# Expert weights in 16 KB pieces: neighbouring rows to one partition, and one DMA for each 2 MB slot

## What is computed

```python
def expert_choice_ffn(h, w_router, w1, w3, w2):        # h (1, 256, 1024)
    cap = EC_CAPACITY_FACTOR * N // N_EXPERTS           # 32 tokens for each of 16 experts
    aff = softmax(h @ w_router)
    gate, idx = top_k(swapaxes(aff, 1, 2), cap)
    xg = h[bidx, idx]                                   # (16, 32, 1024)
    a = einsum('becd,edf->becf', xg, w1)                # w1, w3: (16, 1024, 2048)
    b = einsum('becd,edf->becf', xg, w3)
    ye = einsum('becf,efd->becd', silu(a) * b, w2) * gate   # w2: (16, 2048, 1024)
    return zeros_like(h).at[bidx, idx].add(ye)
```

## Time and profile before

| what | value |
|---|---|
| median of 3 runs | 2690.86 us |
| lowest and highest | 2688.85 and 2696.54 us |
| the profiled execution | 2689.66 us, of which the span of the trace is 2687.9 us |
| TensorE busy | 2231.6 us (83% of the span) |
| TensorE weight loads | 1647.2 us (61%) |
| VectorE, ScalarE, GpSimd busy | 633.4, 588.1, 860.6 us |
| DMA | 680.04 MB, mean 253 GB/s |
| issue to landing of a 1 MB expert load, median | 23.1 us (to the ring), 20.7 us (to the arena) |

### The profile page before, as it was taken

The page is one execution under the profiler, slowest core; times in us unless marked ns, Lnnn a source line. Parts: engine busy times, 40 slices in busy tenths (PEclk is TensorE's granted clock), DMA queues, the critical chain, the costliest instruction groups (busy, mean ns, idle before and its releaser), DMA issues.

```text
span 2687.9 us, 34816 instructions
## 1 busy us (share of the span) xinstructions
PE 2231.6 (83%) x15124; PEld 1647.2 (61%) x15124; DVE 633.4 (24%) x1233; ACT 588.1 (22%) x656; POOL 860.6 (32%) x211
## 2 busy tenths in 40 slices
PE   6799899766665666766665999998998999998998
PEld 2568666422222222222222998997997998997996
DVE  4213332311111111111113033433112032433111
ACT  1111210000000000000001443533333443443332
POOL 1000000000000000000002765676786766576785
PEclk9889799777778778877786999999999999999999
DMA  9634123699999999999997744465554744455553
GB/s 331 191 135 165 62 77 125 265 418 418 418 418 418 419 416 417 417 419 418 418 418 267 266 147 141 130 177 172 188 182 163 240 148 150 126 169 185 174 187 125
DMA packets 284793, 680.04 MB, mean 253 GB/s; under 512 B 11788, under 2 KB 164374, under 8 KB 251217
## 3 DMA queue, kind: packets, MB, share of 16 engines
q1 hardware_dynamic: 282001, 671.55, 67.3%
q0 software_dynamic: 2400, 6.41, 1.0%
q10 hardware_dynamic: 288, 0.53, 0.1%
HBM read 673.85 MB, written 4.59 MB: 252 GB/s over the span
## 4 chain that ended last, share of the span: by engine, by line
PE 63%; DMA 20%; SPq 10%; DVE 4%; issue 1%; ACT 1%; DVEq 0%; ACTq 0%
PE bank L1607 62%; DMA ring_sb<-w_exp 17%; SPq L571 10%; DMA arena_sb<-w_exp 2%; PE bank L1610 2%; DVE x_sb L951 1%; DVE arena_sb L951 1%; DVE arena_sb L954 1%; DVE x_sb L954 1%; DMA ring_sb<-w_in 1%; DMA arena_sb<-hy_skip 0%; DVE x_sb L1450 0%; DMA ring_sb<-w_ada 0%; DVE sm_sb L1438 0%; ACT arena_sb L789 0%
## 5 line engine op out<-in xcount | busy, mean ns | idle before, releaser
L658 POOL TENSOR_TENSOR ring_parts<-ring_sb,ring_parts 128x2048 fp32r<-128x2048 f32 x186 | 849.5, 4576 | 1463.1 <-ACT ring_parts L844 1462.6
L1607 PE MATMUL bank<-hT_parts,ring_parts 128*128 128x256 f32 x3520 | 648.0, 286 | 5.9 <-DVE arena_parts L951 5.9
L1607 PE MATMUL bank<-arena_parts,ring_parts 128*128 128x256 f32 x2672 | 611.2, 284 | 0.0
L1607 PE MATMUL bank<-ring_sb,arena_sb 128*32 128x512 f32 (+2 forms) x2848 | 410.6, 682 | 203.2 <-DMA ring_sb<-w_exp 188.8
L1607 PE MATMUL bank<-arena_sb 128*32 128x256 f32 (+10 forms) x3038 | 434.7, 478 | 161.2 <-DMA arena_sb<-w_exp 121.6
L1607 PEld LDWEIGHTS bank<-hT_parts,ring_parts 128*128 128x128 f32 x3520 | 556.8, 194 | 9.0 <-DVE arena_parts L951 7.5
L1607 PEld LDWEIGHTS bank<-arena_sb 128*128 128x128 f32 (+4 forms) x3038 | 256.4, 172 | 325.6 <-DMA arena_sb<-w_exp 165.0
L1607 PEld LDWEIGHTS bank<-arena_parts,ring_parts 128*128 128x128 f32 x2672 | 450.9, 193 | 0.5 <-issue 0.5
L844 ACT CAST ring_parts<-ring_sb 128x2048 fp32r<-128x2048 f32 x186 | 350.3, 1887 | 270.6 <-DMA ring_sb<-w_ffn_down 66.9
L1607 PEld LDWEIGHTS bank<-ring_sb,arena_sb 128*32 128x32 f32 (+1 forms) x2848 | 112.6, 136 | 478.9 <-DMA ring_sb<-w_exp 293.6
L951 DVE TENSOR_TENSOR arena_sb<-bank,arena_sb 128x512 f32<-128x512 f32 (+5 forms) x205 | 127.2, 643 | 939.8 <-PE bank L1607 875.5
(11 more groups left out here) (208 smaller groups left out, 1022.9 us busy)
## 6 DMA issues: line engine op xcount, KB each, us to landing
ring_sb<-w_exp SPq DMA_DIRECT2D x256, 1024.0 KB, 23.1
arena_sb<-w_exp SPq DMA_DIRECT2D x128, 1024.0 KB, 20.7
ring_sb<-w_in SPq DMA_DIRECT2D x112, 1024.0 KB, 5.3
ring_sb<-w_ada SPq DMA_DIRECT2D x24, 1024.0 KB, 14.1
ring_sb<-w_ffn_gate SPq DMA_DIRECT2D x22, 1024.0 KB, 5.3
ring_sb<-w_ffn_up SPq DMA_DIRECT2D x22, 1024.0 KB, 5.3
ring_sb<-w_ffn_down SPq DMA_DIRECT2D x22, 1024.0 KB, 4.8
ring_sb<-w_ret_proj SPq DMA_DIRECT2D x16, 1024.0 KB, 5.9
```

The lines of the kernel that those rows point to most:

```text
L658: g.tensor_tensor(low, half(n)[0], high.bitcast(F32), ALU.subtract).then_inc(s["lo_ready"], 1)
L1607: return M.matmul(o, l, r, start=first, stop=last)
```

## The change

All three expert tensors go to the partitions in another order. Of w1 and w3, rows 8p to 8p + 7 go to partition p, so that a slot holds two neighbouring rows, 16 KB in one piece; the next partition's piece lies 64 KB further in memory. Of w2, slot r holds rows 512r + 4p to 512r + 4p + 3 in partition p, 16 KB in one piece, and the slot as a whole is 2 MB of memory without a gap. Each slot is one DMA, and the semaphore's counts are halved.

The sums over features stay the same only if the other operand comes in the same order. So the reads on TensorE take a stride: `gather` and `h2T` read `xn2` at every eighth feature, the transposes of `hact` at every fourth, and the halves of `ada_turn` that feed this layer at every eighth. The router's weights are loaded in the same order (one 512-byte piece to a partition), and two rows of constants are put in that order ahead of the launch.

```diff
-        E1 = a["w_exp1"][0].rearrange("e (k p) f -> e p k f", p=P)
-        E3 = a["w_exp3"][0].rearrange("e (k p) f -> e p k f", p=P)
-        E2 = a["w_exp2"][0].rearrange("e (k p) f -> e p k f", p=P)
+        E1 = a["w_exp1"][0].rearrange("e (p k) f -> e p k f", p=P)
+        E3 = a["w_exp3"][0].rearrange("e (p k) f -> e p k f", p=P)
+        E2 = a["w_exp2"][0].rearrange("e (r p c) f -> e r p c f", p=P, c=4)
...
-                w, r = ((E1, c), (E3, c - 4), (E2, c - 8))[c // 4]
                 n = 2 if c < 8 else 4
-                src = w[e, :, n * r:n * r + n]
-                m = n // 2
-                for h in range(2):
-                    sp.dma_start(expert_slot(c, n)[:, h * m:(h + 1) * m],
-                                 src[:, h * m:(h + 1) * m]).then_inc(expert_landed[c % XRING], 16)
+                src = E2[e, c - 8] if c >= 8 else (E1, E3)[c // 4][e, :, 2 * (c % 4):2 * (c % 4) + 2]
+                sp.dma_start(expert_slot(c, n), src).then_inc(expert_landed[c % XRING], 16)
...
-                             (w_router, a["w_router"][0].rearrange("(k p) c -> p k c", p=P)),
+                             (w_router, a["w_router"][0].rearrange("(p k) c -> p k c", p=P)),
...
-                    ins = mm(b[:, 2 * c:2 * c + 2], adarow[:, c // 4, (c % 4) * P:(c % 4 + 1) * P], selsum[:])
+                    row = adarow[:, 2 * (c // 8):2 * (c // 8) + 2].rearrange("p a b -> p (a b)")
+                    by_rows = 2 * batch + c // 8 in (3, 4)
+                    ins = mm(b[:, 2 * c:2 * c + 2], row[:, c % 8:D:8] if by_rows else row[:, (c % 8) * P:(c % 8 + 1) * P], selsum[:])
...
-            turn("h2T", xn2)
+            for i in range(4):
+                b = open_unit("h2T", i)
+                for j in range(2):
+                    for t in range(2):
+                        ins = tr(b[:, j * T + t * P:j * T + t * P + P], xn2[:, t, 2 * i + j:D:8])
+                close(ins)
...
-                        ins = mm(bank[1][:, d * CAP:(d + 1) * CAP], xn2[:, t, d * P:(d + 1) * P], sel[:, t], t == 0, t == 1)
+                        ins = mm(bank[1][:, d * CAP:(d + 1) * CAP], xn2[:, t, d:D:8], sel[:, t], t == 0, t == 1)
...
-                    pe.wait_ge(expert_landed[c % XRING], 32 * (c // XRING + 1) + e * (32 * PER_EXPERT // XRING))
+                    pe.wait_ge(expert_landed[c % XRING], 16 * (c // XRING + 1) + e * (16 * PER_EXPERT // XRING))
...
-                    ins = tr(bank[2][:, c * P:(c + 1) * P], hact[:, c * P:(c + 1) * P])
+                    ins = tr(bank[2][:, c * P:(c + 1) * P], hact[:, c:512:4])
```

More of the change, by code:

```diff
@@ L1919, in expert @@
                     m = 8 + r
-                    pe.wait_ge(expert_landed[m % XRING], 32 * (m // XRING + 1) + e * (32 * PER_EXPERT // XRING))
+                    pe.wait_ge(expert_landed[m % XRING], 16 * (m // XRING + 1) + e * (16 * PER_EXPERT // XRING))
                     w = expert_slot(m, 4)
@@ L2194 @@
     b_in, b_in_2 = arrays["b_in"][0], arrays["b_in_2"]
+    by_rows = lambda v: v.reshape(-1, P, KD).transpose(0, 2, 1).reshape(-1, P)
+    b_ada = rows["b_ada"].reshape(6, D)
+    rows["b_ada"] = np.concatenate([b_ada[0:3].reshape(-1, P), by_rows(b_ada[3:5]), b_ada[5:6].reshape(-1, P)])
+    rows["norm_ffn_g"] = by_rows(rows["norm_ffn_g"])
     packs = {
```

## The result

The changed kernel takes 2672.35 us in the median of 6 runs (2667.63 to 2673.97), the kernel before 2691.65 us in the median of 6 (2685.78 to 2703.37). The ratio is 0.9919, with a 95% interval from 0.9899 to 0.9939: 19 us faster, and clear of the 0.3% that a change must pass to be told from none. The forecast was 2670 us, in a range of 2664 to 2685. The profiled execution of the changed kernel took 2673.63 us, with a span of 2671.8 us.

The account below looks back on a forecast made before the run. The expert stage was taken as bound by the 16 DMA engines' pace through bytes and pieces. -23.2 + 3 = -20.2 us from 2689.66 gives 2669.5; with 1.2 us for the median 2670.7, said as 2670 us, range 2664 to 2685.

Parts of the forecast that it names:

- the line: Expert stage: a 2 MB slot takes 4.824 us plus 9.3 ns for each piece an engine moves.
- 16 KB pieces: Expert stage: 4.898 us a slot, saving 9.0 us on w1 and w3 and 14.2 on w2, -23.2 us.
- Rival A: Expert loads: nothing won beyond 8 KB pieces, so -6.5 us in sum, 2684 us; chance 0.13.
- One DMA for a slot: SyncE's issues of expert loads: 192 fewer, but no landing moves, 0 us.
- The strided reads ahead of the stage: TensorE's 80 loads in h2T, gather(0) and one turn's worth of ada_turn: +3 us, between 0 and +13.9.
- paces part of these: gather(0), 0.220 against 0.113 us a product: something besides the load paces part of the 13.9 us, hiding slower loads.
- rival B: Strided stationary blocks on TensorE load at half pace: +13.9 us, -9.3 us in sum, 2682 us; chance 0.13.
- the +3 us: Cost taken for strided reads ahead of the experts, a fifth of the +13.9 us upper bound.
- The gathers in the loop: gather(e + 1) in the expert loop: even 10.3 us instead of 5.14 is covered by queued loads, 0 us.
- Behind the stage: Chain after the last landing: nothing of the change in it, so all the stage saves is handed on.
- C: w1 and w3 pieces 64 KB apart meet in one part of memory: slower, up to +43 us, 2734 us; chance 0.10.
- D: Something behind the expert stage gives the saving back, leaving around 2690 us; chance 0.06.

Follow-up runs that it names:

- the gapless slots: Changed kernel with slot c of w1 and w3 holding rows 256c + 2p and 256c + 2p + 1, TensorE reading at stride two: 2671.31 us, ratio 0.9920.
- the pitch of 1 MB: Changed kernel with w1 and w3 read 1 MB apart from partition to partition instead of 64 KB, for timing alone: 2673.04 us in one run.

## Why the prediction was right, by its own steps

**The bound.** The stage was bound by the DMA engines, and stays so: share 1.02 before the change and 1.01 behind it. Its length, with the 3.9 us taken from the kernel before, followed the line in nine other versions, within 0.7 us, from 914 to 984 us.

**16 KB pieces.** Forecast 4.898 us a slot and -23.2 us; measured 4.895 us in the slots shown and -23.9 us in the stage of two single executions. The line read from 2, 4 and 8 KB held at 16 KB. Rival A (nothing beyond 8 KB) would have left 4.97 us.

**One DMA for a slot.** Forecast 0, measured 0 (0.9991, and the same stage to 0.1 us).

**The strided reads ahead of the stage.** Forecast +3 us between 0 and 13.9. In the rows of the changed kernel, `gather(0)` is 7.82 us instead of 7.03, turning `xn2` 3.33 instead of 3.27, the second batch's turn 7.33 instead of 6.97, and the third's 7.17 instead of 3.63: +4.8 us; in two other versions with the same strides the third took 6.01 and 5.83 us, which makes 3.4 to 3.6 us. So the size was right. But its reason was only half right. A strided block starts every 7.70 / 32 = 0.24 us at both clock levels; a contiguous one every 0.113 us at 2.4 GHz and every 0.22 us at 1.2 GHz, which was the granted clock (0.50) in `gather(0)` both before and after. TensorE's windows show it, with the number of products in parentheses and the granted clock behind it. The first row is `gather(0)` of the changed kernel, the second lies in its gather(1):

```profile
504.00:512.00 8.00, 7.77 (x32) 0.50 0.01 2
533.00:535.00 2.00, 2.00 (x10) 1.00 1.04 442
```

The same in the kernel before, `gather(0)` and gather(1):

```profile
497.00:503.00 6.00, 6.00 (x30) 0.50 0.01 3
524.00:526.00 2.00, 2.00 (x20) 1.00 1.03 410
```

In 2 us at 2.4 GHz stand 10 strided products against 20 contiguous ones. What "paces part of these" was the clock, and rival B's doubling is true at the high clock and nearly nothing at the low one. So the +3 us, taken as a fifth of the bound without a row for it, came right in part by luck: it rests on `gather(0)` running at 1.2 GHz. At 2.4 GHz its 32 blocks alone would have cost 32 x (0.24 - 0.113) = 4 us, by estimate from these rows, instead of 0.8. The rule on lines in the Trainium skill ("SBUF — State Buffer", "Door 1: The DMA port swizzle") says that every access to a new line pays. The stride of eight floats agrees with it at 2.4 GHz, 0.24 against 0.113 us; at 1.2 GHz hardly anything of the price is left, 0.24 against 0.22. With a stride of two floats (8 bytes), which the rule has free, a block takes 0.120 us against 0.114: nearly so.

**The 8.6 us at the start of the profiled execution** are more than that, and about half of them is not the change. 4.2 us of them are there at 95.70 us, where a group stands that begins at 91.53 us in the kernel before, and up to there no read has a stride. What differs is the granted clock: from 66 to 80 us it is 0.50, and 0.64 in the kernel before. Over the ten profiled executions the stage started between 505.2 and 521.4 us; the four with a stride of eight had 516.8, 514.9, 508.7 and 513.6, the six others 508.2, 505.2, 514.9, 518.9, 521.4 and 508.2. The stride can't be seen in these, and a single profile can't price anything of a few us that stands ahead of the stage. The means differ by 0.7 us (513.5 and 512.8), far less than the spread. So the start itself neither confirms nor refutes the +3 us; the rows of the single steps are what it rests on. With them the sum closes: -23.9 + 3.4 to 4.8 is -20.5 to -19.1 us, and the medians differ by 19.3.

**The gathers in the loop.** Forecast up to 5 us of lateness, hidden behind the queue. They got 0.8 to 4.0 us longer (5.14 to 7.70 in the rows shown), and the stage is the same to 0.1 us with and without the stride. One sentence of the prediction has this the wrong way round: that the waits on weights fall by less than the saving if the gathers get longer. In a stage that the DMA engines bound, more work of TensorE takes the place of its waits, and they fell by 53 us where the stage fell by 24.

**Behind the stage.** Everything was handed on: 1240.1 to 1242.7 us from the last slot's start to the end in all ten (1241.5 before, 1240.8 changed).

**The rivals.** A is refuted by the rate, B by the rows above (in its size, not in its mechanism at the high clock), C by the gapless slots and, in one run, by the pitch of 1 MB, D by the tail. The table in the Trainium skill ("DMA: Bandwidth & Descriptors", "Latency and other measured facts") begins at 512 KiB with a loss of 3%, for copies within the main memory; here loads to the core at 1 MB lost nothing.

## What to carry to other kernels

Where the DMA engines are busy all the time, read the time of equal amounts of data at each piece size that the trace has, and draw the line through them: the slope is the price of a piece, and what longer pieces can give can be estimated before a line of code is written, as can the end of it (here 4.824 us of 4.895 do not depend on the pieces by the line, so 1.5% is all that is left; no piece over 16 KB was tried). Where weights can be laid out so that a partition's share is one run, the sum over features can follow them by a strided read on TensorE, which cost nothing here while TensorE had slack, or by a strided write elsewhere. A share of the chain in the issuing queue is not yet a bound: with one DMA for two it went from 10% to 1%, and the time stayed.

## What the runs showed of the hardware that I had not expected

SyncE stood in the issue of expert loads before the change, 1.09 us in the median to the ring and up to 4.6 us, while after it each issue takes 0.33 us and never over 0.43. With one DMA for two and pieces as before, an issue still takes up to 8.97 us. With w2 alone at 16 KB it is never over 0.47 us, and with 2 KB pieces it is 2.3 us in the median to the ring and up to 8.9. With two DMAs a slot and 8 KB pieces everywhere it is up to 3.79 us. The issues to the arena (ns, minimum, median and maximum) in the versions with one DMA for two, with two DMAs and 8 KB pieces, and with w2 alone:

```profile
L569 SPq DMA_DIRECT2D arena_sb<-w_exp x64: 372/1044/8970, 469.5 to 1418.4; - x64
```

```profile
L570 SPq DMA_DIRECT2D arena_sb<-w_exp x128: 327/456/3791, 478.9 to 1415.9; - x128
```

```profile
L568 SPq DMA_DIRECT2D arena_sb<-w_exp x64: 327/352/471, 479.1 to 1412.5; - x64
```

Fewer pieces in the queue go with shorter issues, and halving the number of DMAs alone did not end the long ones. But the number of pieces is not the whole of it: six slots of w1 and w3 hold 6 x 256 pieces in the last two of these versions alike, and only the one with two DMAs a slot was held up. What the limit is was not settled. It cost nothing here, since loads were always queued.

The load of a 128 x 128 stationary block at a stride of eight floats takes the same time at both clock levels, 0.24 us, so its price over a contiguous block depends on the clock: 0.13 us at 2.4 GHz, 0.02 us at 1.2 GHz.
